# Weight units loaded into the place of their low part, by the queue of the stores, in a two-layer streaming encoder

## The reference

```python
# layer A
u = rmsnorm(x, norm_a) @ w_in_a;  xb, gate = split(u)          # 1024 -> 2048
xc = causal_conv4(xb) ;  i, r = sigmoid(block_diag(xc, w_gx)), sigmoid(block_diag(xc, w_ga))
a = exp(8 * r * log_sigmoid(lam));  h = scan(a, sqrt(1 - a*a) * i * xc)
x1 = x + (h * silu(gate)) @ w_out_a
# shared keys and values
k, v = split(rmsnorm(x1, norm_kv) @ w_kv);  k = rmsnorm_per_head(k)
# layer B: 16 heads, 2 kv heads, window of 128 in chunks of 64, sinks
q, gate = split(rmsnorm(x1, norm_b) @ w_in_b);  q = rmsnorm_per_head(q)
y = x1 + (attention(q, k, v, sink) * silu(gate)) @ w_out_b
```

## Time and profile before

| | us |
|---|---|
| median of 3 runs | 1641.98 (1640.94 to 1642.12) |
| profiled execution, its own time | 1643.85 |
| its span | 1642.1 |
| PE busy | 1533.2 (93%) |
| DVE busy | 1175.5 (72%) |
| ACT busy | 707.2 (43%) |
| POOL busy | 394.9 (24%) |

### The profile page before, as it was taken

The page is one execution under the profiler, slowest core; times in us unless marked ns, Lnnn a source line. Parts: engine busy times, 40 slices in busy tenths (PEclk is TensorE's granted clock), DMA queues, the critical chain, the costliest instruction groups (busy, mean ns, idle before and its releaser), DMA issues.

```text
span 1642.1 us, 30977 instructions
## 1 busy us (share of the span) xinstructions
PE 1533.2 (93%) x10611; PEld 1443.7 (88%) x10611; DVE 1175.5 (72%) x2355; ACT 707.2 (43%) x1568; POOL 394.9 (24%) x306
## 2 busy tenths in 40 slices
PE   6899999998789999998799999999996899999999
PEld 5799999998679999998788999999994688878888
DVE  6964854857489999999865737647457877777771
ACT  5322212223876766773334424334335444434440
POOL 4310000034675555555341000000231111111110
PEclk9999999999889999999999999999998999999999
DMA  5431211233233333333543112122433343333412
GB/s 179 126 119 62 80 66 66 79 109 122 90 115 98 106 104 105 106 103 94 158 109 119 58 57 85 49 70 71 125 100 101 99 112 98 100 89 90 114 46 77
DMA packets 160801, 158.25 MB, mean 96 GB/s; under 512 B 53680, under 2 KB 153776, under 8 KB 160688
## 3 DMA queue, kind: packets, MB, share of 16 engines
q1 hardware_dynamic: 142544, 119.86, 24.6%
q0 software_dynamic: 7776, 28.32, 5.7%
q10 hardware_dynamic: 10368, 8.66, 1.6%
HBM read 102.68 MB, written 54.36 MB: 96 GB/s over the span
## 4 chain that ended last, share of the span: by engine, by line
PE 47%; DVE 17%; issue 6%; ACT 3%; DMA 3%; SPq 1%; DVEq 0%; POOL 0%; ACTq 0%; POOLq 0%
PE s_banks L588 19%; PE bank L1380 11%; DVE r_th L862 4%; PE s_banks L1318 3%; DVE r_x_hi L886 3%; PE bank L1333 2%; PE bank L1363 2%; PE bank L1121 2%; PE bank L1335 2%; PE bank L1366 2%; DMA b_x<-x_dram 1%; PE bank L573 1%; DVE r_x L882 1%; PE s_banks L1090 1%; PE bank L588 1%
## 5 line engine op out<-in xcount | busy, mean ns | idle before, releaser
L632 POOL TENSOR_TENSOR w_lo_a<-w_raw,w_hi_a 128x1024 fp32r<-128x1024 f32 x28 | 67.6, 2414 | 615.6 <-ACT w_hi_a L627 615.6
L1550 ACT ACTIVATE m_p<-s_banks,m_nm 128x192 f32<-128x192 f32 (+2 forms) x264 | 106.1, 414 | 191.9 <-DVE m_nm L1431 191.9
L1380 PE MATMUL bank<-m_y_hi,w_hi_a 128*128 128x256 f32 (+1 forms) x512 | 149.8, 293 | 0.6 <-DVE m_out L1481 0.6
L1380 PE MATMUL bank<-m_y_lo,w_hi_a 128*128 128x256 f32 (+1 forms) x512 | 144.9, 283 | 0.0
L1380 PE MATMUL bank<-m_y_hi,w_lo_a 128*128 128x256 f32 (+1 forms) x512 | 144.8, 283 | 0.0
L588 PE MATMUL bank<-a_hi,w_hi_a 128*128 128x352 f32 x384 | 127.8, 333 | 15.4 <-DVE w_lo_a L632 11.4
L588 PE MATMUL s_banks<-b_hi,w_hi_a 128*128 128x352 f32 x384 | 130.5, 340 | 0.0
L1597 POOL TENSOR_TENSOR m_y_lo<-m_y,m_y_hi 128x256 fp32r<-128x256 f32 x66 | 48.6, 736 | 329.2 <-DVE m_y_hi L1473 329.2
L588 PE MATMUL bank<-a_hi,w_lo_a 128*128 128x352 f32 x384 | 125.7, 327 | 0.0
L588 PE MATMUL bank<-a_lo,w_hi_a 128*128 128x352 f32 x384 | 125.7, 327 | 0.0
L588 PE MATMUL s_banks<-b_hi,w_lo_a 128*128 128x352 f32 x384 | 124.2, 323 | 0.0
(11 more groups left out here) (198 smaller groups left out, 4889.1 us busy)
## 6 DMA issues: line engine op xcount, KB each, us to landing
w_raw<-weights_dram POOLq DMA_DIRECT2D x54, 512.0 KB, 4.1
a_x<-xT_dram SPq DMA_DIRECT2D x48, 176.0 KB, 2.3
xc_dram<-a_out SPq DMA_DIRECT2D x48, 176.0 KB, 1.9
sga_dram<-a_out SPq DMA_DIRECT2D x48, 176.0 KB, 1.8
r_xc<-xc_dram SPq DMA_DIRECT2D x32, 264.0 KB, 3.0
r_sg<-sga_dram SPq DMA_DIRECT2D x32, 264.0 KB, 2.7
r_x<-xT_dram SPq DMA_DIRECT2D x64, 132.0 KB, 2.2
x_dram<-r_x SPq DMA_DIRECT2D x64, 132.0 KB, 1.8
```

Source lines behind the costliest of these rows:

```text
L632: ops.tensor_tensor(low, raw[:, u % 2, :], high.bitcast(F32), ALU.subtract).then_inc(w_split, 1)
L1380: mm = nc.tensor.matmul(out_bank(ts, blk)[:, 0:width], w[pw][:, kt * P:(kt + 1) * P], (m.y_hi, m.y_lo)[px][tp][:, kt, 0:width], start=(n = ...
L1550: nc.scalar.activation(m.p[:, q, k, v0:192], s_banks[:, 2 * q + e, bp * 192 + v0:(bp + 1) * 192], ACT.Exp, bias=m.nm[:, q, k:k + 1], accum ...
```

## The change

1. The two raw buffers go. A second name (`w_raw_a`, `w_raw_b`, `w_raw_c`) lies on the place of each low part; a unit is loaded there, rounded into the high place, and the low part is written over it. A load can thus start only when the slot's last use is over.
2. The loads leave GpSimd's queue for SP's, where the stores are. At the start SP issues unit 0, the constants `vec`, inputs 0, 2, 4, unit 1, input 6 and then units 2 to 9; ScalarE's queue issues inputs 1, 3, 5, 7 and the other constants. Later loads stand behind the stores of their slots: in the last step of `a1` and `b1` behind the store of the slot that frees the place, four loads at slot 0 of the last recurrence step, one behind each of the last tile's eight residual stores, and four before the stores of the states. 12 semaphores (LOADS) count landings.
3. In the last step of `a1` and `b1` ScalarE's high part of a unit moves from one slot to two slots behind the slot that frees it. The first two of layer B's units move from slot (RN, 0) to (RN, 1).
4. Step 0: ScalarE rounds all eight inputs with units 0, 1, 2 between them, and squares afterwards with units 3 and 4 between the squares; VectorE makes all eight low parts with those of units 0 and 1 between them, and adds the squares afterwards (`add_input`). VECTOR_UNITS is 2: units 2 and 3 go to GpSimd. `a1` has two buffers for squares. TensorE's sum over the squares stands after slot 2 of the first step and no longer after slot 0.
5. The negation of the sinks moves behind VectorE's step 0, and the waits for constants are split into `vec_loaded` and `const_loaded`.

```diff
+LOADS = 12
...
         w_hi_a = sb("w_hi_a", [P, SLOTS_A, D], F32R)
+        with ExitStack() as own:
+            w_raw_a = tensors(own)("w_raw_a", [P, SLOTS_A, D])
         w_lo_a = sb("w_lo_a", [P, SLOTS_A, D], F32R)
-        raw = sb("w_raw", [P, 2, D])
...
-                    m.sq, m.acc = b(f"{tag}_sq", [P, 1, PT]), b(f"{tag}_acc", [P, 1, PT])
+                    m.sq, m.acc = b(f"{tag}_sq", [P, 2, PT]), b(f"{tag}_acc", [P, 1, PT])
...
-            need(eng, m.sq_added, n)
-            nc.scalar.activation(m.sq[:, 0, :], m.x[:, blk % nx, :], ACT.Square).then_inc(m.sq_done, 1)
+
+        def square_input(eng, m, s, blk):
+
+            nx, nq, n = m.x.shape[1], m.sq.shape[1], NB * s + blk
+            need(eng, m.sq_added, n + 1 - nq)
+            nc.scalar.activation(m.sq[:, blk % nq, :], m.x[:, blk % nx, :], ACT.Square).then_inc(m.sq_done, 1)
...
+                    if isinstance(s, int) and s == 0:
+                        if j % 2 == 0 and j < NB:
+                            load_input(eng, m, s, j)
+                        if j == 4:
+                            load_unit(eng, m.unit + 1)
+                        if j >= NB:
+                            load_unit(eng, m.unit + 2 + j - NB)
+                    elif known(s, 0, PN - 1) and j < NB:
                         load_input(eng, m, s, j)
+                    if isinstance(s, int) and m.first_weights and s == 1 and j < 2 * NB - 10:
+                        load_unit(eng, m.unit + 10 + j)
...
+                    if isinstance(s, int) and s == PN and next_unit(m, j) is not None:
+                        load_unit(eng, next_unit(m, j), m.proj_done, 2 * NB * (PN - 1) + j + 1)
...
+            if m.first_weights:
+                for blk in range(NB):
+                    high_input(eng, m, 0, 0, blk)
+                    if blk % 3 == 0:
+                        high_part(eng, m.unit + blk // 3)
+                for blk in range(NB):
+                    square_input(eng, m, 0, blk)
+                    if blk in (2, 5):
+                        high_part(eng, m.unit + 2 + (blk + 1) // 3)
...
+            if m.first_weights:
+                for blk in range(NB):
+                    low_input(eng, m, 0, 0, blk)
+                    if blk == 0 or blk == 3:
+                        low_part(eng, nc.vector, m.unit + blk // 3)
+                for blk in range(NB):
+                    add_input(eng, m, 0, blk)
+                eng.wait_ge(const_loaded, 16 * N_CONST)
+                nc.vector.tensor_scalar(neg_sink[:, :], sink[:, :], -1.0, None, ALU.mult).then_inc(const_made, 1)
...
-                    if j == 0:
+                    if j == (2 if first else 0):
...
-        VECTOR_UNITS = 4
-
-        def load_unit(eng, u):
-            need(eng, w_split, u - 1)
-            eng.dma_start(raw[:, u % 2, :], A["weights"][u, :, :]).then_inc(raw_loaded[u % 2], 16)
+        VECTOR_UNITS = 2
+
+        def split(eng, u):
+
+            if u < VECTOR_UNITS:
+                eng.wait_ge(w_split_first, u + 1)
+            else:
+                eng.wait_ge(w_split, u - VECTOR_UNITS + 1)
+
+        def load_unit(eng, u, freed=None, count=0):
+
+            if freed is not None:
+                eng.wait_ge(freed, count)
+            if u >= LOADS:
+                split(eng, u - LOADS)
+            eng.dma_start(slot_of(u)[2], A["weights"][u, :, :]).then_inc(raw_loaded[u % LOADS], 16)
...
-        def high_part(eng, u, freed=None, count=0):
-
-            eng.wait_ge(raw_loaded[u % 2], 16 * (u // 2 + 1))
-            if freed is not None:
-                eng.wait_ge(freed, count)
-            nc.scalar.activation(slot_of(u)[0], raw[:, u % 2, :], ACT.Copy).then_inc(w_high, 1)
+        def high_part(eng, u):
+
+            high, _, raw = slot_of(u)
+            eng.wait_ge(raw_loaded[u % LOADS], 16 * (u // LOADS + 1))
+            nc.scalar.activation(high, raw, ACT.Copy).then_inc(w_high, 1)
 
         def low_part(eng, ops, u):
-            high, low = slot_of(u)
+            high, low, raw = slot_of(u)
             eng.wait_ge(w_high, u + 1)
-            ops.tensor_tensor(low, raw[:, u % 2, :], high.bitcast(F32), ALU.subtract).then_inc(w_split, 1)
+            ops.tensor_tensor(low, raw, high.bitcast(F32), ALU.subtract)\
+               .then_inc(w_split_first if u < VECTOR_UNITS else w_split, 1)
 
         def low_units(eng, first, end):
 
             for u in range(first, end):
-                if u >= VECTOR_UNITS:
-                    low_part(eng, nc.gpsimd, u)
-                if u + 2 < UNITS:
-                    load_unit(eng, u + 2)
+                low_part(eng, nc.gpsimd, u)
...
-            if m.first_weights and s == 0 and j in (0, 2, 4, 6, 8):
-                return (m.unit + j // 2,)
             if m.first_weights and s == 1 and j + 5 < 2 * NB:
-                return (m.unit + 5 + j,)
+                return m.unit + 5 + j
             if not m.first_weights and s == 1 and 1 <= j <= 7:
-                return m.unit + 8 + j, r.kv_mm, NB * RN
-            if s == PN and j:
-                last_use = SLOTS_IN_B if m.heads else list(range(2 * NB))
-                for k in range(m.next_units):
-                    if j == last_use.index(SLOTS_OUT_B[k] if m.heads else k) + 1:
-                        return m.unit + 2 * NB + k, m.proj_done, 2 * NB * (PN - 1) + j
+                return m.unit + 8 + j
+            if s == PN and j >= 2:
+                u = next_unit(m, j - 2)
+                return u if u is not None and u < m.unit + 2 * NB + m.next_units else None
             return None
 
+        def next_unit(m, j):
+
+            last_use = SLOTS_IN_B if m.heads else list(range(2 * NB))
+            k = last_use[j]
+            if m.heads:
+                return U_OUT_B + SLOTS_OUT_B.index(k) if k in SLOTS_OUT_B else None
+            return U_GATE + k if k < SLOTS_A + SLOTS_B else None
...
+            def load_next(pair, q):
+                t, blk = pair[0], pair[1] + q
+                if isinstance(t, int) and t == RN - 1:
+                    load_unit(eng, U_B1 + UNITS_GATE + blk, r.out_done, NB * t + blk + 1)
...
+                    if isinstance(s, int) and (s, g) == (RN, 0):
+                        for k in range(UNITS_GATE):
+                            load_unit(eng, U_B1 + k, r.gates_done, 4 * NG * RN)
                     if pair:
                         store_x1(pair, 0)
+                        load_next(pair, 0)
...
+            for u in range(U_B1 + UNITS_GATE + UNITS_OUT_A, U_OUT_B):
+                load_unit(eng, u, r.kv_mm, NB * RN)
...
+            load_unit(eng, 0)
+            eng.dma_start(vec[:, :, :], A["vec"]).then_inc(vec_loaded, 16)
...
+            for blk in range(1, NB, 2):
+                load_input(eng, a1, 0, blk)
+            eng.dma_start(sink[:, :], A["sinks"]).then_inc(const_loaded, 16)
+            eng.dma_start(halo[:, :, :], conv0).then_inc(const_loaded, 16)
+            eng.wait_ge(vec_loaded, 16)
```

More of the change, by code:

```diff
@@ L141, in build @@
         w_hi_b = msb("w_hi_b", [P, SLOTS_B, D], F32R)
+        with ExitStack() as own:
+            w_raw_b = tensors(own)("w_raw_b", [P, SLOTS_B, D])
         w_lo_b = msb("w_lo_b", [P, SLOTS_B, D], F32R)
@@ L187, in project_memory @@
             m.silu_done = sem(f"{tag}_silu_done")
[L188 to L193, removed]
+            if heads:
+                m.q2_done = sem(f"{tag}_q2_done")
+                m.qms_done = sem(f"{tag}_qms_done")
+                m.qstd_done = sem(f"{tag}_qstd_done")
+                m.qrec_done = sem(f"{tag}_qrec_done")
+                m.q_normed = sem(f"{tag}_q_normed")
+            else:
                 m.halo_read, m.conv_step, m.conv_done = sem(f"{tag}_halo_read"), sem(f"{tag}_conv_step"), sem(f"{tag}_conv_done")
@@ L368, in low_input @@
                 eng.wait_ge(m.sq_added, n)
-                nc.vector.tensor_tensor(m.acc[:, 0, :], m.acc[:, 0, :], m.sq[:, 0, :], ALU.add)\
+                nc.vector.tensor_tensor(m.acc[:, 0, :], m.acc[:, 0, :], m.sq[:, blk % nq, :], ALU.add)\
                   .then_inc(m.sq_added, 1)
         def run_project(eng, m, body):
-            if m.first_weights:
+            if m.first_weights and eng is not nc.scalar and eng is not nc.vector:
                 body(0, 0)
@@ L438, in body @@
                     unit = project_unit(m, s, j)
-                    if unit:
-                        high_part(eng, *unit)
+                    if unit is not None:
+                        high_part(eng, unit)
                     after(s, j)
+            if m.first_weights:
[7 more added lines that the diff above has]
+                        high_part(eng, m.unit + 2 + (blk + 1) // 3)
             run_project(eng, m, body)
@@ L489, in continue_input @@
                     low_input(eng, m, s, par, blk)
-                unit = project_unit(m, s, j)
-                if unit and unit[0] < VECTOR_UNITS:
-                    low_part(eng, nc.vector, unit[0])
+                    add_input(eng, m, s, blk)
```

(27 more changed lines are left out.)

43 lines of the change are left out of this document (24 added, 19 removed).

## The result

The changed kernel takes 1665.67 us (median of 4 runs, 1664.56 to 1666.87) against 1642.05 of the kernel before in the same session (1640.94 to 1645.24): ratio 1.0135, 95% interval 1.0122 to 1.0149. It is slower by 23.6 us in the medians, where +5.5 was forecast, and outside the range. The profiled execution's span went from 1642.1 to 1665.1 us, 23.0 more.

A forecast was written before the change was run, and what follows sets the result against it. TensorE was taken as full in the projection steps and losing time at the seams. Terms 0.0 + 2.6 + 1.7 + 0.1 + 1.9 - 0.8 = +5.5 us on 1641.98 gave 1647.5 us, range 1637 to 1655.

The forecast's parts named there:

- the hand-over to attention: Second projection to attention: the last unit's later low part holds VectorE's m_nm to 1233.9, +1.9 us (bound +0.5).
- slower, 0.51: Whole kernel: the chance given to a slower time; same had 0.22, faster 0.27.
- The start: Kernel start: first matmul 3.3 us earlier, first reciprocal at 26.0 instead of 25.76; sum 0.0, bounds -2.7 and +2.5 us.
- lost to the same VectorE stretch: Start: the 9 us TensorE gains at its first unit go again in VectorE's full stretch.
- The hand-over to the recurrence: First projection to recurrence: unit 22's low part delays the first xc_lo, TensorE resumes at 395.0, half hidden; +2.6 us.
- The last recurrence step: Recurrence's last step: four loads ahead of small transfers delay the load of x; +1.7 us, bounds 0 and +3.
- the second rival: Loads don't hold the small transfers at the last recurrence step and state stores: +0.3, 1642.3 us; chance 0.20.
- The hand-over to the second projection: Recurrence to second projection: state stores land 5.35 us late, faster inputs offset it; +0.1, bounds -3.4 and +2.8 us.
- 1 for the clock: Second projection's first step: 1 us allowed for the clock in TensorE's end at 895.7, before 895.6.
- GpSimd without issues: GpSimd: low parts run back to back without load issues, three pairs on the path; -0.8 us, bounds -2 and 0.
- The first rival: VectorE's two full stretches hold fewer low parts, each worth 2.05 to 2.2 us; five fewer give 1637; chance 0.27.
- SP as the bound: SP's loads behind residual stores each add 1.4 us to the load of x behind: 1654.5 us; chance 0.11.

The follow-up runs named there:

- e2: Changed kernel with the first six output units' high parts at slots 3 to 8 of ScalarE's order, not 2 to 7: 1641.73 us, 0.9986 of before.
- e1: Changed kernel with the first six output units' high parts at slots 8 to 13 of ScalarE's order, not 2 to 7: 1641.21 us, 0.9984 of before.
- e3: Changed kernel with SP's load for slot j+2 ahead of the store of slot j in the second projection's last step: 1640.52 us, 0.9978 of before.
- e12: Changed kernel with the first three output units' high parts left at slots 2 to 4, the next three at 11 to 13: 1654.23 us, 1.0064 of before.
- e4: Changed kernel with unit 22's low part behind the recurrence's first low part on GpSimd: 1663.98 us, 1.0116 of before.
- e9: e6 with only the state stores moved ahead of the last four loads on SP: 1635.31 us, 0.9949 of before.
- e6: Changed kernel with the edits of e3 and e4 joined: 1639.59 us, 0.9976 of before.
- e10: e8 plus the low parts of units 2 to 4 on VectorE: 1637.96 us, 0.9960 of before.
- e8: e6 with slot (RN, 0)'s four loads at that slot's end and state stores ahead of the last four loads: 1632.87 us, 0.9930 of before.

## Why the prediction was wrong, step by step

**The step that failed** is the hand-over to attention, +1.9. It looked at the last unit only. The prediction had worked out for the first projection that a load now waits for "the store in front of it on SP", and took the second projection's last step to behave alike. There it doesn't. In `a1` the store waits for the branch of its own slot, and ScalarE has nothing behind the high part that a branch needs; in `b1` the store waits for a head that is normalized three slots late, while the high part stands two slots late and the roots stand behind it. Because 2 is less than 3, the high part of unit j stands ahead of the root of head j+1, and a turn passes only one head; at three slots (e2) it passes two. Experiments e1, e2, e3 and e12 show it four ways: two by ScalarE's order, one by the queue, one by half the dose. The term measured +25.2 (the ring with its gains, and the hold of `m_nm`).

That the time went the way the forecast leaned (slower, 0.51) is luck: no term and no rival held the ring, and without it (e1, e2, e3) the changed kernel is 0.1 to 0.2% faster than the one before.

The term's own content was right, but hardly a cost. `m_nm` was held by the last low part; timelines of VectorE and GpSimd, after, in answer to the earlier trace rows:

```profile
1256.32 1.88 DVE L1501 TENSOR_TENSOR m_nm<-m_nmax,neg_sink 128x4 f32<-128x4 f32 x1
```

```profile
1255.85 2.34 POOL L691 TENSOR_TENSOR w_lo_a<-w_raw_a,w_hi_a 128x1024 fp32r<-128x1024 f32 x1 [0.25 <-ACT w_hi_a L686]
```

From the last reciprocal of `b1` to the end e1, whose `m_nm` took 2.36 us, needs 471.9 us, e2 (1.88 us) 471.5, and e3 (0.32 us) 472.0. So the hold shows no price of its own at the end, though two profiles of one kernel differ by 2.4 us in this stretch.

**The start**, 0.0: measured -0.6 at the end of the first projection, by another way. VectorE's timeline, in answer to the earlier trace rows:

```profile
14.01 2.47 DVE L376 SCALAR_TENSOR_TENSOR a_lo<-a_x,vec,a_hi 128x352 fp32r<-128x352 f32 x1 [0.15 <-ACT a_hi L363]
...
18.64 3.69 DVE L389 TENSOR_TENSOR a_acc<-a_acc,a_sq 128x352 f32<-128x352 f32 x3 [0.63 <-ACT a_sq L370]
22.97 3.07 DVE L389 TENSOR_TENSOR a_acc<-a_acc,a_sq 128x352 f32<-128x352 f32 x2 [0.64 <-ACT a_sq L370]
...
27.58 2.35 DVE L538 RECIPROCAL a_std<-a_std 128x352 f32<-128x352 f32 x1 [1.46 <-ACT a_std L444]
```

The last input held by unit 2's low part and the adds held by those of units 3 and 4 are as forecast (until 16.5, not 15.1). x0 was used at 6.90, not 5.2, so all stands 1.6 us later: the reciprocal missed its 26.0 by that. (The terms given for it, 24.55 + 0.7 + 0.55, add up to 25.8.) TensorE then waits 6.0 us for a free bank, as "lost to the same VectorE stretch" says. Eight low parts lie in that stretch, as counted. The 2.4 us come back behind it, in the first step: the last branch is not held, and where TensorE before waited 2.52 us and ran at a mean clock of 0.63 from 77 to 80 us, it now waits 0.49 us and has 1.00.

**The hand-over to the recurrence**, +2.6: the mechanism is right, the chain of the changed kernel in answer to the earlier trace rows:

```profile
389.61 2.34 POOL w_lo_a L691
391.95 1.26 POOL r_xc_lo L1102
393.21 0.14 issue
393.35 5.00 PE s_banks L1160 x24
```

Forecast 395.0, because the branches ended at 386.8 and not at 388.2. Relative to its own start the seam cost 3.4, and half of it was hidden as forecast: 1.7 are left at 748 us (1.16 and the 0.57 by which the step began earlier). e4 took them back: its last `r_std` reciprocal ahead of 750 us comes 2.0 us earlier.

**The last recurrence step**, +1.7. The loads do hold the small transfers, SP's timeline in answer to the earlier trace rows:

```profile
755.55 1.84 SPq L667 DMA_DIRECT2D w_raw_a<-weights_dram  x4
757.44 0.73 SPq L810 DMA_DIRECT2D x_dram<-r_x  x1
764.08 0.33 SPq L805 DMA_DIRECT2D r_x<-xT_dram  x1
```

The load of x waits 6.6 us for the store in front of it, and VectorE adds x at 766.76, 3.5 us after the earlier trace rows. That settles the second rival against itself. But the loss is gone at the end of the step: -0.4. In the experiments the step takes 77.8 to 81.9 us against 80.6, with the loads in either place. So it hides such a delay, or it is too small to be seen among these differences.

**The hand-over to the second projection**, +0.1: measured 0.0. The state stores landed at 844.14 (forecast near 845), the input behind them came in 2.6 us. That is 3.9 us later than before and not 5.35; the two terms named for it, 1.8 and 5.5, give neither. And no row stood behind the "1 for the clock": from 830 to 860 us the mean was 0.94 before and 0.83 after. This looks like the best hit, and hid the most. The later landing was set against the gain from inputs that no weight slows, and need not be spent at all: in e9 the state stores land at 839.0, the input behind them still comes in 3.1 us, and the time is 4.3 us below that of e6.

**GpSimd without issues**, -0.8: one stretch fits it. Between the last two `r_std` reciprocals lie 32.7 to 32.9 us in the three profiles of the old order and 31.6 to 32.3 in the eleven of the new one; that the missing issues are the cause is not shown. The first rival fell: six low parts lay inside the branches of the last step, as counted. Of the others, SP as the bound comes nearest in size (1654.5, still 11 us short), but for the wrong reason: the time was lost not in issues but in what one of them stood behind.

## What to carry to other kernels

When a load moves into a queue with stores, write down for each load what the store ahead of it waits for, and for each consumer of the load what stands behind it on its engine; if the second list leads back to the first, count the turn of the ring and how many steps one turn passes. This ring cost its turn (8.8 us) less the step it replaced (4.4), once for each time around; one slot more of distance cost nothing here and returned 24 us (e2). And put the small transfer whose landing releases an engine ahead of the large one that nobody awaits yet.

## What the hardware showed that was not expected

- Around and behind a wait of TensorE of 4.8 us the mean granted clock was 0.68 and 0.98 in two windows of 10 us, around one of 2.1 us 1.00 and 1.00; the step took 73.0 and 68.0 us. In e10 an earlier start of 3 us was lost within one step, with a longer wait (3.35 us against 1.62) and a lower clock (0.89 against 1.00).
- A stall of VectorE of 2.6 to 3.7 us that waits for nothing shown comes at the same reduce in five of fourteen profiles, twice alike in the same kernel, and each time with three packets of an instruction queue around it, of which the nine others have none there. Such a stall is 0.2% of this kernel, and the stretch behind `m_nm` differs by 2.4 us between two profiles of one kernel: a difference of that size between two kernels needs no cause in the change.
- Behind four loads of 512 KB a store on the same queue took 6.6 us until the next transfer could go; with the loads behind it (e8), 1.8 us.
